# Merge gates beside early attention, and merge to routing in sections of two token tiles

## What is computed

```python
o_sb, o_nsa, o_moba = ...                                    # from x @ w_in
g = jax.nn.sigmoid(merge_g).reshape(B, S, N_BRANCHES, D)     # merge_g: 3 x 1024 columns of x @ w_in
mix = g[:, :, 0] * (o_sb @ w_br_sb) + g[:, :, 1] * (o_nsa @ w_br_nsa) + g[:, :, 2] * (o_moba @ w_br_moba)
x = layer_norm(DEEPNORM_ALPHA * x + mix @ w_out, ln1_g, ln1_b)
# peer_ffn: q = x @ w_q; scores against two sets of 128 keys, top 8 of each, top 8 of the 64 sums, per head (4)
act = jax.nn.gelu(jnp.einsum('thkd,td->thk', u_tab[idx], xb))
y = jnp.einsum('thk,thkd->td', (g * act), v_tab[idx])
x = layer_norm(DEEPNORM_ALPHA * x + y, ln2_g, ln2_b)
```

## Time and profile before

| | before |
|---|---|
| median of the runs shown | 3162.5 us (3154.18 to 3178.01) |
| time of the profiled execution | 3160.5 us |
| its span, first to last instruction | 3158.7 us |
| mean granted clock of TensorE | 0.819 |
| ScalarE, GpSimd busy | 720.2 us (23%), 1251.9 us (40%) |
| moved by DMA | 701.19 MB, 222 GB/s on average |

### The profile page before, as it was taken

The page is one execution under the profiler, slowest core; times in us unless marked ns, Lnnn a source line. Parts: engine busy times, 40 slices in busy tenths (PEclk is TensorE's granted clock), DMA queues, the critical chain, the costliest instruction groups (busy, mean ns, idle before and its releaser), DMA issues. The chain is left out here.

```text
span 3158.7 us, 26039 instructions
## 1 busy us (share of the span) xinstructions
PE 2485.8 (79%) x8728; PEld 1216.3 (39%) x8728; DVE 2026.7 (64%) x4136; ACT 720.2 (23%) x1506; POOL 1251.9 (40%) x1028
## 2 busy tenths in 40 slices
PE   7889989878898998988799778988897887656000
PEld 4434434433333443453244334533332756534000
DVE  0231121557888666558877877478888757678888
ACT  2450001234444010124411001233434111000000
POOL 0000000114546442315675634135656533665575
PEclk9589999967779999995699889856668999888555
DMA  3001121436768674657898967357877867998697
GB/s 158 31 1 60 60 80 73 161 117 219 230 210 280 239 278 168 239 192 248 276 330 299 345 244 273 144 153 249 258 234 277 324 258 295 355 346 305 237 344 291
DMA packets 164581, 701.19 MB, mean 222 GB/s; under 512 B 18400, under 2 KB 18400, under 8 KB 156384
## 3 DMA queue, kind: packets, MB, share of 16 engines
q0 software_dynamic: 147456, 536.94, 49.2%
q1 hardware_dynamic: 14256, 152.28, 12.5%
q10 hardware_dynamic: 2736, 10.31, 0.8%
HBM read 691.07 MB, written 8.39 MB: 221 GB/s over the span
## 5 line engine op out<-in xcount | busy, mean ns | idle before, releaser
L467 POOL DMA_INDIRECT rows<-in_table_u,idx x512 | 618.9, 1209 | 1343.5 <-DVE idx L1154 701.1
L467 POOL DMA_INDIRECT rows<-in_table_v,idx x512 | 632.8, 1236 | 548.8 <-DVE y L1061 409.1
L508 PE MATMUL ps<-xT,wring 128*128 128x512 f32 (+1 forms) x1920 | 697.0, 517 | 71.8 <-DVE scratch L1197 31.4
L1061 DVE SCALAR_TENSOR_TENSOR y<-rows,wts,y 128x1024 f32<-128x1024 f32 x512 | 657.0, 1283 | 85.4 <-DMA rows<-in_table_v,idx 45.4
L1047 DVE CUSTOM_DVE_ANT_0 rows<-rows,x 128x1024 f32<-128x1024 f32 x512 | 614.9, 1223 | 66.0 <-DMA rows<-in_table_u,idx 63.2
L508 PEld LDWEIGHTS ps<-xT,wring 128*128 128x128 f32 x1920 | 370.7, 195 | 383.1 <-issue 304.5
L670 PE MATMUL ps<-KA,QA 33*128 33x512 f32 (+7 forms) x576 | 336.2, 722 | 52.3 <-DVE negm L1297 31.1
L522 PE MATMUL ps<-wring,scratch 128*128 128x512 f32 x512 | 231.8, 616 | 68.0 <-DVE scratch L1197 37.3
L1193 DVE SCALAR_TENSOR_TENSOR scratch<-scratch,ps 128x512 f32<-128x512 f32 (+1 forms) x120 | 69.5, 579 | 266.0 <-ACT scratch L824 266.0
L543 PE MATMUL ps<-xT,wring 128*128 128x512 f32 (+1 forms) x640 | 229.2, 520 | 10.4 <-issue 6.6
L704 PE MATMUL ps<-QA,KA 64*128 64x512 f32 x408 | 227.6, 842 | 7.5 <-ACT scratch L947 7.4
(11 more groups left out here) (168 smaller groups left out, 2243.3 us busy)
## 6 DMA issues: line engine op xcount, KB each, us to landing
wring<-in_merge SPq DMA_DIRECT2D x30, 2304.0 KB
wring<-in_w_out_h SPq DMA_DIRECT2D x10, 2048.0 KB
wring<-in_w_query SPq DMA_DIRECT2D x10, 2048.0 KB
x_row<-in_x SPq DMA_DIRECT2D x16, 512.0 KB
wring<-in_attn_a SPq DMA_DIRECT2D x4, 2048.0 KB
rows<-in_table_u,idx POOLq DMA_INDIRECT x512
rows<-in_table_v,idx POOLq DMA_INDIRECT x512
x_row<-x_mid SPq DMA_DIRECT2D x16, 512.0 KB
```

The source lines that it names most:

```text
L467: pool.indirect_dma_start(rows[:, n % GATHER_SLOTS, :], None, tab_u if first_half else tab_v, bass.IndirectOffsetOnAxis(ap=idx[:, GT * (g ...
L508: pe.matmul(bank(k % 4)[:, 0:W], wg[:, c, P * c4:P * (c4 + 1)], xT[:, c, toks], start=(c == 0), stop=(c == KC - 1))
L1061: v.scalar_tensor_tensor(out=y[:, :], in0=row, scalar=wts[:, t, e:e + 1], in1=y[:, :], op0=ALU.mult, op1=ALU.add).then_inc(row_used, 1)
```

## The change

- **Gates early.** The 24 gate pieces of a group, without their branch matmuls, are cut into four parts of two matmuls each and stand as steps ("gate") in phases 0 to 2 of attention: 9, 8 and 7 in groups 0 and 2; 6, 9 and 9 in groups 1 and 3. They accumulate in bank 6; ScalarE copies each into a new tile `G` (3 x 8 x 512 columns). The sticks have two banks instead of three for it.
- **Sections of two tiles.** Every group now has two sections. Section 0 (tiles 0 and 1) stands in pieces in phases 3 and 4: tanh, merge, output projection and the first half of the norm in phase 3; second half of the norm, turns, query, match and routing in phase 4. Its merge and output pieces use bank 6 alone, the rest banks 0 and 1. Section 1 (tiles 2 and 3) follows densely with four banks. Tanh is taken over the stored gates, three operations of 2048 columns per section. `w_out` and `w_query` are loaded for each section.
- **Expert steps.** Per section 32 u steps and 32 v steps tile by tile (u, u, v, v). `expert_shares` places them with a running model of TensorE and VectorE (1.45 us per step). Before the first merge of section s all steps up to section s - 2 plus 12 must be done. y is summed in x1 in place (x1 is not scaled first; the gates are divided by `ALPHA`), the ends of a tile (norm, gelu) come some steps later, and stores have a semaphore per tile.
- **Loads.** Items of `wring` are 256 columns wide for each of eight chunks (1 MB, rows of 1 KB). All four x tiles of the next group are loaded during section 1. The residual is loaded anew into `xT`, in rows of 128 columns, once the gates are done. `ln1` is loaded per section into `G`. The identity is loaded before the other constants.
- Freed: `x_row`, `y`, `ck_sh`, `cv_sh`, `ln1_gb` now lie in `scratch`, `x1`, `KA` or `G`.

```diff
+ST = 2
+NS = GT // ST
+SECTIONS = [(g, s) for g in range(NG) for s in range(NS)]
+ITEM = KC * 256
+RING = 2
+GATES = 24
+GATE_PARTS = 4
+GATE_SPLIT = ((9, 8, 7), (6, 9, 9))
...
+def gate_steps(half, phase):
+    lo = sum(GATE_SPLIT[half][:phase])
+    return [("gate", k, part, 1.72) for k in range(lo, lo + GATE_SPLIT[half][phase]) for part in range(GATE_PARTS)]
+def section_steps(s):
+    first = [("tanh", s, 0, 4.0)] + [("merge", s, k, 0.9) for k in range(12)]
+    for k in range(2 * ST):
+        first += [("out", s, (k, part), 1.72) for part in range(4)]
+        if k >= ST:
+            first.append(("mean", s, k - ST, 0.0))
+    second = []
+    for tt in range(ST):
+        second += [("norm", s, tt, 7.0)] + [("turn", s, 2 * tt + c, 1.5) for c in range(2)]
+    second += [("query", s, (j, part), 1.72) for j in range(4) for part in range(4)]
+    second += [("match", s, k, 1.2) for k in range(2 * ST)]
+    return first, second + [("route", s, tt, 1.0) for tt in range(ST)]
 def merged_steps(half):
...
+        if phase < 3:
+            streams.append((gate_steps(half, phase), 1.0))
+        else:
+            streams.append((section_steps(0)[phase - 3], (0.9, 0.75)[phase - 3]))
...
-    return out
+    return out + sum(section_steps(1), [])
...
+        if what is not None and what[:3] == ("merge", what[1], 0) and sec >= NS:
+            nxt = max(nxt, SECTION_STEPS * (sec - NS + 1) + 12)
+            busy += EXPERT_US * (nxt - lo)
+        if what is not None and what[0] == "norm":
+            busy += 0.5
+        busy = max(busy, now) + dve
+        now += pe
+        while nxt < ready and max(busy, started) + EXPERT_US <= now + EXPERT_AHEAD:
+            busy = max(busy, started) + EXPERT_US
+            nxt += 1
+        now = max(now, busy - EXPERT_AHEAD)
...
+        if what is not None and what[0] == "route" and what[2] == ST - 1:
+            ready, started = SECTION_STEPS * (sec + 1), busy + 8.0
+EXPERT_US, EXPERT_AHEAD = 1.45, 3.0
...
+        def piece(sec, kind, k):
+            if SECTIONS[sec][1] > 0:
+                return bank(k % 4)
+            return bank(6 if kind in ("merge", "out") else k % 2)
...
+                for k in range(GATES // 2):
+                    load(head_item(g, 4 + k), columns(w_merge[layer, 3 * (k % 4 // 2) + k // 4], 256 * (k % 2), 256 * (k % 2 + 1)))
...
+                        elif a == 0:
+                            pe.wait_ge(gate_copied, k)
+                        for c in range(KC * a // GATE_PARTS, KC * (a + 1) // GATE_PARTS):
+                            mm = pe.matmul(bank(6), wg[:, c, P * (t % 2):P * (t % 2 + 1)], xT[:, c, :],
+                                           start=(c == 0), stop=(c == KC - 1), skip_group_check=True)
...
-                        pe.matmul(bank(4 + M % 3), k_sb[:, P * (i - a):P * (i - a + 1)],
+                        pe.matmul(bank(4 + M % 2), k_sb[:, P * (i - a):P * (i - a + 1)],
...
+                if kind == "tanh":
+                    nc.scalar.preload_act_table_set("exp_and_others")
+                    act.wait_ge(gate_copied, GATES * (g + 1))
+                    for b in (2, 1, 0):
+                        raw = G[:, b, :, toks]
+                        nc.scalar.activation(raw, raw, ACT.Tanh, scale=0.5).then_inc(gate_sig, 1)
+                    nc.scalar.preload_act_table_set("natural_log_exp_and_others")
...
+                if e == 12 and sec != BLOCKS[b - 1][0]:
+                    expert_gates(sec)
+                if e == 6 and b > 0:
+                    expert_finish(b - 1)
...
                 dve.wait_ge(scores_copied, 2 * (T + 1))
+                dve.wait_ge(values_done, pairs_before(GT * g + GT - 1) + 1)
```

More of the change, by code:

```diff
@@ L177, in merged_steps @@
             out.append(("done", phase - 1, 0, 0.5))
-    return out
+    return out + sum(section_steps(1), [])
 STEPS = [merged_steps(half) for half in range(2)]
+SECTION_KINDS = ("tanh", "merge", "out", "mean", "norm", "turn", "query", "match", "route")
 ROW_KINDS = ("zc", "score", "turn_c", "chosen", "shift")
@@ new lines, in points, with expert_shares @@
+def points():
+    out = []
+    for g in range(NG):
+        out += [("proj", g, n) for n in range(6)]
+        out += [("step", g, n) for n in range(len(STEPS[g % 2]))]
+    return out
+def expert_shares():
+    out, now, busy, nxt, ready, started = {}, 0.0, 0.0, 0, 0, 0.0
+    for kind, g, n in points():
+        lo = nxt
+        what = STEPS[g % 2][n] if kind == "step" else None
+        pe, dve = cost(g % 2, what) if kind == "step" else (9.5, 0.0)
+        sec = NS * g + what[1] if kind == "step" else 0
+        if what is not None and what[:3] == ("merge", what[1], 0) and sec >= NS:
[9 more added lines that the diff above has]
+        now = max(now, busy - EXPERT_AHEAD)
+        if what is not None and what[0] == "norm" and what[1] == NS - 1:
+            now = max(now, busy)
+        out[(kind, g, n)] = range(lo, nxt)
+        if what is not None and what[0] == "route" and what[2] == ST - 1:
+            ready, started = SECTION_STEPS * (sec + 1), busy + 8.0
+    out["rest"] = range(nxt, ALL_STEPS)
+    return out
```

872 lines of the change are left out of this document (446 added, 426 removed).

## The result

The kernel after takes 3258.4 us (median; 3243.9 to 3262.6), the kernel before beside it 3163.4 us: ratio 1.0295, 95% interval 1.0248 to 1.0342. It is slower by 3%; 3047 us were forecast, with 2870 to 3210 as the range. Its profiled span is 3242.0 us.

The account below looks back on a forecast made before the run. No engine was full: they take turns, and attention loses time to idling and a slow clock. Groups of 568, 759, 618 and 759 us (2704), a tail of 341 and 2 between span and time gave 3047 us; range 2870 to 3210.

Parts of the forecast that it names:

- Gates into early attention: 24 gates per group, 165 us, move under attention and fill its waits; one-bank waits cost 12 us per group.
- The loss that stays: Attention's time beyond its work at full clock: 85 us per group, 60 in group 0.
- the prediction's own sign: For the four groups, of about 570, 760, 620 and 760 us: one 40 us off its term means the prediction is wrong.
- The expert steps, the tail: Behind the last routing stand 198 expert steps instead of 128; the tail takes 341 us instead of 256.
- The dense section: Merge to routing of tiles 2 and 3: 130 us in groups 1 to 3, lower bound 105; 95 in group 0.
- DMA: Weight loads, now in rows of 1 KB, cost 4.0 us of all 16 engines per MB, against 2.6 before.
- Head: Start of each group: 70 us, as x rows are loaded a stage earlier; 80 in group 0.
- A: Filling of attention works as planned: loss 56 us (40 in group 0), dense section 105, 2865 us; chance 0.18.
- C: Gain and price cancel: groups 1 and 2 unchanged, group 3 some 800, group 0 at 585, 3123 us; chance 0.14.
- B: Beside the gates, late gathers hold VectorE in its written order and so stall TensorE: +297, 3344 us; chance 0.20.

Follow-up runs that it names:

- a_dense0: The kernel after with the section of tiles 0 and 1 also put behind attention, in four banks; 3247.8 us, ratio 1.0299 to the kernel before.
- a_layout: The kernel after with attn_a, merge, output and query weights laid out as one 8 KB run per partition and item; 3173.5 us, ratio 1.0065.
- a_dma4: The kernel after with the gathers alone cut to a quarter, 256 instead of 1024 columns; 3133.4 us.
- l_fo3: The kernel after with 8 KB weight runs, later forced steps, row loads and norm constants behind output weights, planner's step price 1.3 instead of 1.45 us; ratio 1.0255.

## Why the prediction was wrong, point by point

- **Gates into early attention**: right. The clock there is 0.95 to 0.98, the first gather comes at 502 us (about 470 forecast), TensorE's waits for the gate's one bank are 28 us in the whole kernel against 12 us per group taken, and taking the filling away costs 107 us or more. The rule of the Trainium skill ("TensorE: Matmul & The Clock Gate", section "HAM oscillation") that steady work keeps the clock up agrees with these rows.
- **The loss that stays**: 85 us per large group taken, 90 and 102 measured; 60 in group 0 and 82 measured; 85 in group 2 and 98 measured. Mis-sized by 57 us in sum. Section 0 beside late attention runs at 0.87 to 0.92, and `a_dense0` shows that what it hides is too little to measure. By the prediction's own sign (a group 40 us off its term) groups 0, 2 and 3 fail, at 66, 55 and 46 us over; group 1 is 36 over. TensorE's last work ends at 2907 us, not near 2710.
- **The expert steps, the tail**: right. 335 us against 341.
- **The dense section**: the step that failed, 117 of the 197 us. It was priced as the larger of two loads: TensorE with VectorE's merge (105 us) or the DMA (126 us), at full clock. Measured in group 1: TensorE is busy 91 of 145 us at 0.78, about 71 us of work; it stands 54 us, and the slow clock costs the other 20 (where the same products stand with fewer gaps, in the first section of `a_dense0`, it is 0.88). The DMA is at 0.82, VectorE at 67%. The waits follow each other through a ring of two slots, the forced steps and two norms, and such waits add; the prediction took the largest engine's sum and put them at nothing. The products and merges alone, with no forced steps and no gathers, took 101 us in `a_dense0`, where I had 74 + 14 = 88. Larger packets for the weights take 76 us off the four sections (`a_layout`), quarter gathers 91 us (`a_dma4`); the two overlap, and no run shares the 117 us out. I had the forced steps (17 us), but not that y, the row loads and the output weights hang behind them; loosening that chain gave 0.6%.
- **DMA**: 4.0 us per MB was too dear: 3.09 measured. The prediction quoted the Trainium skill, "DMA: Bandwidth & Descriptors", section "Why small descriptors are slow (HBM only)", for 9% over the beats: 3.09 over 2.82 is 9.5%, which agrees with it closely, and the line through two queues was wrong. But neither led to the 76 us of kernel time, which show as TensorE waiting less for its weights.
- **Head**: 78 to 80 instead of 70 in groups 1 to 3. The rows are there early, as said, and the head's own products take some 65 us (1429 to 1494 in group 2); but the first gate weight waits for the slot of the compressed projection, and TensorE stands 14 to 16 us for it behind them.
- **The rivals**: A's filling came and its 105 us sections did not. C's stages were nearest (585, and groups 1 and 2 as now): group 0 came to 634 and group 2 to 673. The time is on B's side, but B's mechanism does not make it: VectorE waited 97 and 34 us for gathers in the whole kernel, not several hundred, and the stage that B had stalling, the gates beside attention, is the one that ran well. `l_fo3` shows that B is near: with 12% more steps beside the gates that stage grows by 32 us.

## What to carry to other kernels

Price a stage that stands alone by its chain, not by its fullest engine: list what each in-order queue has ahead of the item that TensorE needs next, and add the waits, with the clock that such gaps leave. Splitting a dense stage in two doubles the loads of its weights, and here it left the groups as long as before although the filling of early attention paid 107 us; 70 more steps in the tail then made the kernel 95 us slower. When a wait is removed and the time stands still, look at what the released engine waits for next, in the queue that issues its loads.

## What I had not expected of the hardware

- Loads with runs of 1 KB instead of 8 KB per partition cost 9.5% in DMA engine time (3.09 against 2.82 us per MB) and 18 to 20 us in each dense section, which takes eleven items in turn through two slots.
- Four gather slots of 512 KB instead of six: 422 us for 198 steps and the routing, against 335, and 258 GB/s against 307.
- The granted clock in the dense sections, where TensorE was busy 55 to 65% of the time with gaps of 3 to 24 us, was 0.75 to 0.81; in the mixture with late attention, busy 81 to 88%, it was 0.87 to 0.92.
- The same two-tile section took 101 us with no gathers and no expert steps beside it and 163 us with them (`a_dense0`, group 1), though no engine was full in either.
